# Latent attention on one core: two scores between the projections, transposes and scores alternating, modulation rows between head pairs

## The reference

```python
h = x @ w_in
c_q, c_kv, k_rope = h[..., :384], h[..., 384:640], h[..., 640:]
q = (rmsnorm(c_q, q_a_gain) @ w_q_up).reshape(B, S, 16, 96)
kv = (rmsnorm(c_kv, kv_a_gain) @ w_kv_up).reshape(B, S, 16, 128)
k_nope, v = kv[..., :64], kv[..., 64:]
k = concatenate([k_nope, broadcast(k_rope)], -1)
q, k = rmsnorm(q, q_gain), rmsnorm(k, k_gain)
# the last 32 of the 96 columns of q and k are rotated by position
o = causal_attention(q, k, v)          # softmax over 256 keys
return o.reshape(B, S, 1024) @ w_out
```

## Time and profile before

| | us |
|---|---|
| median of 3 runs | 2492.74 |
| lowest and highest | 2491.65, 2496.98 |
| the profiled execution | 2491.8 |
| its span in the trace | 2490.2 |

### The profile page before, as it was taken

One profiled execution on the slowest core, in us unless ns is written; L12 is line 12 of the kernel. 1 busy time (PEld: TensorE's weight loads), 2 busy tenths in 40 slices (PEclk: granted clock), 3 DMA queues, 4 the chain that ended last, 5 costly groups with the idle time before them and its releaser, 6 DMA issues.

```text
span 2490.2 us, 37770 instructions
## 1 busy us (share of the span) xinstructions
PE 2313.0 (93%) x16663; PEld 2103.8 (84%) x16663; DVE 1218.8 (49%) x1517; ACT 971.6 (39%) x1153; POOL 509.9 (20%) x453
## 2 busy tenths in 40 slices
PE   6999999989999998889999899979999989888998
PEld 6998889879999997567999877867888877667997
DVE  5645566656555553445555355362133264445444
ACT  3433344444433342334444344333222233534442
POOL 2112434312211111220221111012202210230220
PEclk9999999999999998779999999989999999999999
DMA  6555434355555555676554310113332222213551
GB/s 243 176 173 174 140 119 136 124 198 173 183 178 183 182 176 185 212 253 226 181 186 153 110 35 18 35 68 102 101 102 90 97 97 85 68 51 98 179 182 68
DMA packets 205245, 344.72 MB, mean 138 GB/s; under 512 B 8845, under 2 KB 69498, under 8 KB 205082
## 3 DMA queue, kind: packets, MB, share of 16 engines
q1 hardware_dynamic: 205082, 342.31, 41.5%
HBM read 341.24 MB, written 1.05 MB: 137 GB/s over the span
## 4 chain that ended last, share of the span: by engine, by line
PE 77%; DVE 10%; POOL 6%; ACT 4%; issue 3%; SPq 0%; DMA 0%; DVEq 0%; POOLq 0%; ACTq 0%
PE PS L467 74%; PE PS L476 3%; DVE WL L453 3%; POOL small L1504 1%; ACT WH L440 1%; POOL small L1502 1%; POOL TMP L1513 1%; DVE rstd L588 1%; DVE XL L635 1%; DVE TMP L1430 1%; DVE small L1408 0%; DVE XL L1003 0%; DVE al L999 0%; POOL TMP L1514 0%; DVE TMP L1435 0%
## 5 line engine op out<-in xcount | busy, mean ns | idle before, releaser
L453 DVE TENSOR_TENSOR WL<-raw,WH 128x2048 fp32r<-128x2048 f32 (+2 forms) x281 | 651.5, 2331 | 724.5 <-ACT WH L440 724.5
L467 PE MATMUL PS<-XH,WH 128*128 128x256 f32 (+1 forms) x2336 | 699.6, 299 | 40.3 <-issue 15.3
L467 PE MATMUL PS<-XL,WH 128*128 128x256 f32 (+1 forms) x2336 | 693.5, 297 | 0.0
L467 PE MATMUL PS<-XH,WL 128*128 128x256 f32 (+1 forms) x2336 | 693.3, 297 | 0.0
L440 ACT ACTIVATE WH<-raw 128x2048 fp32r<-128x2048 f32 (+2 forms) x281 | 518.8, 1858 | 360.5 <-PE PS L467 360.0
L467 PEld LDWEIGHTS PS<-XH,WH 128*128 128x128 f32 x2336 | 452.1, 194 | 56.8 <-issue 18.5
L467 PEld LDWEIGHTS PS<-XL,WH 128*128 128x128 f32 x2336 | 453.0, 194 | 10.1
L467 PEld LDWEIGHTS PS<-XH,WL 128*128 128x128 f32 x2336 | 452.8, 194 | 10.0
L467 PE MATMUL PS<-WH,XH 128*128 128x256 f32 (+2 forms) x944 | 287.8, 305 | 19.3 <-DVE XL L635 8.3
L467 PE MATMUL PS<-WH,XL 128*128 128x256 f32 (+2 forms) x944 | 279.3, 296 | 0.0
L467 PE MATMUL PS<-WL,XH 128*128 128x256 f32 (+2 forms) x944 | 279.2, 296 | 0.0
(11 more groups left out here) (236 smaller groups left out, 2574.0 us busy)
## 6 DMA issues: line engine op xcount, KB each, us to landing
raw<-in_ffn_w_in SPq DMA_DIRECT2D x88, 1024.0 KB, 5.1
raw<-in_w_mod SPq DMA_DIRECT2D x48, 1024.0 KB, 5.2
raw<-in_ffn_w_out SPq DMA_DIRECT2D x40, 1024.0 KB, 4.9
raw<-in_a_w_in SPq DMA_DIRECT2D x36, 1024.0 KB, 4.9
raw<-in_w_mlp_in SPq DMA_DIRECT2D x32, 1024.0 KB, 5.5
raw<-in_w_mlp_out SPq DMA_DIRECT2D x32, 1024.0 KB, 5.0
raw<-in_gla_w_in SPq DMA_DIRECT2D x12, 1024.0 KB, 5.1
raw<-in_attn_w_qkv SPq DMA_DIRECT2D x6, 1024.0 KB, 5.0
```

The costliest lines, as they stand in the source:

```text
L453: dve.e.tensor_tensor(self.WL[j % NRAW][:, 0:nk * nn], self.raw[j % NRAW][:, 0:nk * nn], wh.bitcast(F32), ALU.subtract).then_inc(*self.lo. ...
L467: return self.pe.e.matmul(out, l, r, start=start, stop=stop, skip_group_check=skip)
```

## The change

The four functions are put in another order; no arithmetic is changed and no instruction is added or left out.
- TensorE: in a turn, the scores of heads 0 and 1 go between the query product and the key/value product. Then come softmax transpose 0, score 2, softmax transpose 1, score 3, values 0 and 1, a fill, head transpose of the queries, softmax transposes 2 and 3, a fill, values 2 and 3, head transpose of the keys, a fill. The last turn, without products, has its first fill where the key/value product would be. Softmax transposes have banks of their own (6, 1, 2, 3 by head), head transposes 6 and 1. In the first four turns the small modulation matmuls go to bank 4 in place of 2.
- ScalarE: exponentials 0 and 1 ahead of the keys' squares; both squares ahead of both value copies; each fill's row is copied out where the fill stands.
- VectorE: sums of the queries, scores 0 and 1, scaling of the queries, softmax copies 0 and 1, sums of the keys, scores 2 and 3, rotation of the queries, fill, scaling of the keys and the multiplication of their rotation, softmax copies 2 and 3, the addition of the keys' rotation, fill, reciprocals and output division, fill.
- GpSimd: the sine part of the queries' rotation ahead of the keys' power.

```diff
-    LAT_FILLS = ((1, 3, 5), (0, 2, 4))
+    LAT_FILLS = ((0, 4), (0, 2))
...
         def turn(hs, w):
             for h2 in range(2):
-                b = spare = 7 - spare
+                b = (6, 1)[h2]
...
         def turn_p(hs, hd):
-            b = spare = 7 - spare
+            b = (6, 1, 2, 3)[hd]
...
         for hs in range(-1, 4):            # TensorE
+            more, own = hs < 3, hs >= 0
+            fill = lambda: self.pe_mods.send(self.LAT_FILLS[not more])
             if more:
                 up(w_qu[:, (hs + 1) * 384:(hs + 2) * 384], 0, 3, 384, 0, ("lat", "q", hs + 1))
+            if own:
+                score(hs, 0)
+                score(hs, 1)
+            if more:
                 up(w_kvu[:, (hs + 1) * 512:(hs + 2) * 512], 3, 2, 512, 2, ("lat", "kv", hs + 1))
+            else:
+                fill()
+            if own:
+                turn_p(hs, 0)
+                score(hs, 2)
+                turn_p(hs, 1)
+                score(hs, 3)
+                pv(hs, 0)
+                pv(hs, 1)
+            if more:
+                fill()
+                turn(hs + 1, 0)
+            if own:
+                turn_p(hs, 2)
+                turn_p(hs, 3)
+            fill()
+            if own:
+                pv(hs, 2)
+                pv(hs, 3)
+            if more:
+                turn(hs + 1, 1)
+            fill()
...
         for hs in range(-1, 4):            # VectorE
             if more:
                 self.dve_begin()
                 sums(0, hs + 1)
+            if own:
+                score(hs, 0)
+                score(hs, 1)
+            if more:
+                scaled(0, hs + 1)
+            else:
+                fill()
+            if own:
+                turn_p(hs, 0)
+                turn_p(hs, 1)
+            if more:
                 self.dve_begin()
                 sums(1, hs + 1)
+            if own:
+                score(hs, 2)
+                score(hs, 3)
+            if more:
+                rotate(0, hs + 1)
+                rotated(0, hs + 1)
+                fill()
+                scaled(1, hs + 1)
+                rotate(1, hs + 1)
+            if own:
+                turn_p(hs, 2)
+                turn_p(hs, 3)
+            if more:
+                rotated(1, hs + 1)
+            fill()
...
+            dve.wait_ge(self.expd, ("lat", hs, 3))
+            dve.e.reciprocal(rd, den).then_inc(*self.v_step.up(("lat", "recip", hs)))
             dve.wait_ge(self.weighed, ("lat", hs, 3))
...
             t.then_inc(*self.o_done.up(("lat", hs)))
+            fill()
...
         for hs in range(4):                # GpSimd
             for w in range(2):
                 head_norm(w, hs)
-            for w in range(2):
                 rotate(w, hs)
```

## The result

The changed kernel took 2457.45 us (median of 4 runs, 2455.11 to 2459.6), the kernel before, beside it, 2494.86 (2491.65 to 2498.28): a ratio of 0.985, 95% interval 0.983 to 0.9869. Forecast were 2458.6 us and a ratio of 0.986. The spans of the profiled executions differ by 32.1 us (2490.2 and 2458.1).

What follows compares the result with a forecast made beforehand. TensorE was taken as the bound, losing time in the latent head stage to waits and a clock fallen to 1.2 GHz. Savings of 28.0 + 2.5 + 3.6 = 34.1 us from 2492.7 gave 2458.6 us, range 2453 to 2474.

Steps and rivals of the forecast that it cites:

- Part 1: Three middle groups of the latent head stage: covered waits and full clock shorten them from 101.3 to 73.3 us, saving 28.0.
- margins of 0.1 to 0.3 us: Middle groups: operands for the softmax transposes and bank 2 are ready only 0.1 to 0.3 us before TensorE wants them.
- rival A: Middle groups: some tight waits surface; slips of 0.5 us at four places cost 2 us a group, 2464.6; chance 0.23.
- the second way: Middle groups: waits of 3.5 us plus 5.9 us of slow clock make 9.4 a group, against 9.3 by adding the work.
- The transposes and the clock: Middle groups: a rule says transposes don't count as busy for the clock; the forecast had the clock stay up behind them.
- rival D: Middle groups: clock stays at 1.2 GHz for most of each group, by transposes or small matmuls; 2519 us, chance 0.03.
- Part 2: First products before any scores: shorter first wait, no second wait, clock perhaps rising earlier; saves 2.5 us, bounds 0.7 and 6.
- the 10 of the prediction's signs: Start of the stage: if the forecast is right, low clock is left only in the first 10 us.
- Part 3: Last group and output: new order starts the output product at 21.15 instead of 24.8 us, saving 3.6; bounds 2 and 4.3.
- The two short waits: Last group: TensorE waits 0.5 us each for softmax 2 and softmax 3.
- DMA at nothing: Middle groups: loads cost nothing at some 300 GB/s; without cover a group could not be shorter than 22 us.
- The total: Whole kernel: 34.1 us saved, from 2492.7 to 2458.6 us.

Runs made afterwards that it cites:

- experiment 3: The kernel before, with 18 useless matmuls ahead of softmax transpose 0 of the middle groups; 2489.59 us, ratio 0.9977.
- experiment 4: The kernel before, with 18 useless matmuls ahead of softmax transpose 0 of the middle groups and 18 more behind it; 2483.69 us, ratio 0.9956.
- the second execution: The changed kernel run and profiled again with nothing altered; median 2460.02 us, stage 118.7 us.
- Experiments 8 to 10: Changed kernel with third fill's row in bank 5, 2457.73 us; also VectorE's second output split held back, 2457.75; also 14 useless matmuls in the last turn, 2454.08.
- experiment 1: The changed kernel with scores 0 and 1 of the three middle groups behind the key/value product again on TensorE; 2464.46 us, ratio 0.9872.
- experiment 2: The kernel before, with only scores 0 and 1 moved between the two products on TensorE, ScalarE and VectorE; 2494.34 us, ratio 0.9997.

## Why the prediction was right, point by point

- **Part 1, the walk through a group:** right. Times from the group's start, forecast and measured: softmax transpose 0 at 7.4 (7.26), transpose 1 at 8.5 (8.42), first modulation step at 10.95 (10.81), head transposes at 13.95 (13.79), softmax transposes 2 and 3 at 14.85 (14.70). One of the margins of 0.1 to 0.3 us was used up: from score 2 to softmax transpose 1 it is 0.84 us (1062.73 to 1063.57), where the last group, which waits for no bank there, needs 0.66 (1109.95 to 1110.61), and VectorE's scaling, which frees the bank, ended at 1063.42. This slip of 0.2 us is far below the 0.5 of rival A, which did not come. A group without falls of the clock took 24.6 us where 24.7 was forecast. What was missed is small: the prediction had the clock at full speed in all three groups, and in the first profiled execution two of them began at half clock, 1.5 us each, behind the wait of 0.81 us. The first rows of the third group at half speed, those of the second at full speed above them:

```profile
1055.58 0.52 PE L467 MATMUL PS<-WH,al 128*128 128x384 f32 x2
...
1081.05 0.84 PE L467 MATMUL PS<-WH,al 128*128 128x384 f32 x2
```

- **The split of this gain into waits and clock:** the sum is right both ways, but the second way is no independent proof. Waits of 3.5 us and 5.9 for slow work are how the same 34.1 us of the old group are divided, so they must give what Part 1 gives by adding the work. As the worth of the clock alone, which is how experiments 3 and 4 took the 5.9, it is too much: experiment 4 gives 4.1, and 5.3 for the waits. A wait for VectorE, which runs at its own pace, is longer when TensorE is faster, as experiment 3 shows (1.13 to 2.15 us).
- **The transposes and the clock:** the Trainium skill (TensorE: Matmul & The Clock Gate, Part 4: PE-mode transpose) says that transposes don't count as busy the same way. The second middle group, with 28 transposes between other matmuls, kept the clock at 1.00 in both profiled executions, and in the other groups it fell only at the start, in the query product. In this mix the rule costs nothing, and rival D did not come. The group in the second execution:

```profile
1052.08:1076.71 24.63, 23.81 (x170) 17.22 (x171) 14.84 (x44) 11.50 (x30) 7.20 (x10) 1.00 0.91 313
```

- **Part 2:** 1.9 us against 2.5. Both waits moved as forecast (2.97 to 2.28; 1.24 to none), and the clock fell all the same. From the first modulation product to the first group's start it took 14.96 us in place of 17.20; what was not in the sum is that the query product ahead of it ran longer at half clock in this execution and gave back 1.0 us. In the second execution it didn't, and the turn took 24.94 us, 2.9 less than before. The low clock lasted until 1022.3, some 19 us into the stage, and not the 10 of the prediction's signs. Bank 4 was not tried alone.
- **Part 3:** 4.0 us against 3.6. The two short waits came (0.48 and 0.33 us, forecast 0.5 each), the clock held, and the output product waited for the low half behind two weight splits, as named.
- **DMA at nothing:** right. The middle group moved 308 GB/s at a share of 0.90, and no row of TensorE waited for a load.
- **The total:** 34.1 forecast, 32.1 between the spans, 37.4 between the medians. The difference between the last two is scatter: the profiled execution lay below the median before (2491.8 against 2494.86) and above it after (2459.46 against 2457.45). The single times of both kernels lie in two clusters, near 2492 and 2497 before, near 2455 and 2460 after. That the forecast of 2458.6 came within 1.2 us of the median is therefore in part luck.

Experiments 8 to 10 add a caution: with the same instructions behind the stage, the time there differed by up to 8 us from trace to trace, so the agreement of the totals to about 1 us is better than the method deserves.

## What to carry to other kernels

When several engines feed one another in a fixed order, write down from one traced group when each operand is ready and when the bound engine comes for it, and move work until every readiness lies ahead of its use; the single moves may each be worth nothing, as the scores moved alone were. Price waits for another engine by that engine's clock, not by the length that the wait has now. And judge a gain of a few microseconds by the stage's own time in the trace: the total may take it back, or add to it, in a stage that was never touched.

## What the runs showed of the hardware that I had not expected

- TensorE's clock fell to 1.2 GHz behind a wait of 0.81 us in two of three groups of one execution, where the small matmuls with 2 columns and a modulation product stood ahead of the wait, and in none of another execution of the same kernel. In the ten traces that have this wait ahead of their three middle groups, it fell in 10 of 30.
- Behind waits of 1.30 us, with the wide products of a projection and two scores ahead of them, it held in three of three groups (experiment 1); behind 2.41 us, with the same ahead, it fell in three of three. Yet in experiment 2 the product behind a wait of 2.92 us ran at full clock, and the fall came with the next wait of 2.05 us, in three of three. The length of a wait alone does not decide.
- Once fallen, it stayed down for some 13 us of nearly unbroken work in the old middle groups, through small matmuls, scores and values, with one wait of 1.13 us among them.
- Kernels with the same instructions behind the stage took from 1080.8 to 1088.6 us there, for the most part by the clock in a mixer a thousand microseconds later; two kernels whose stages differ by 0.3 us differed by 4.1 us behind it.
